# A layer's first panels: the third low part ahead of the folding of the squares, the ones-matmul and the turn of the roots one panel later

## What is computed

```python
def rms_norm_2(x, gain, eps=NORM_EPS):
    xf = x.astype(jnp.float32)
    y = xf * lax.rsqrt(jnp.mean(xf * xf, axis=-1, keepdims=True) + eps)
    return (y * gain.astype(jnp.float32)).astype(x.dtype)
...
    h = x
    for l in range(DEPTH_2):
        u = rms_norm_2(h, attn_norm[l])
        proj = jnp.einsum('bsd,dc->bsc', u, w_in[l])
        (dq, dk, dv, rq, rk, rv, rg, gq, gk, gv, gate_logits) = split_cols(proj, IN_SPLITS)
...
        h = h + jnp.einsum('bsd,de->bse', merged, w_out[l])
        m = jnp.einsum('bsd,df->bsf', rms_norm_2(h, mlp_norm[l]), w_mlp_in[l])
        m = jnp.square(jax.nn.relu(m))
        h = h + jnp.einsum('bsf,fd->bsd', m, w_mlp_out[l])
```

## Time and profile before

| | |
|---|---|
| time, median of 3 runs | 2093.12 us (2092.78 to 2095.03) |
| time of the profiled execution | 2092.37 us |
| its span | 2090.3 us |
| TensorE busy | 1963.7 us, 94% of the span |
| VectorE, GpSimd, ScalarE busy | 54%, 29%, 19% |
| mean granted clock of TensorE | 0.982 |

### The profile page before, as it was taken

One profiled execution on the slowest core, in us unless ns is written; L12 is line 12 of the kernel. 1 busy time (PEld: TensorE's weight loads), 2 busy tenths in 40 slices (PEclk: granted clock), 3 DMA queues, 4 the chain that ended last, 5 costly groups with the idle time before them and its releaser, 6 DMA issues.

```text
span 2090.3 us, 33307 instructions
## 1 busy us (share of the span) xinstructions
PE 1963.7 (94%) x13854; PEld 1776.9 (85%) x13854; DVE 1133.7 (54%) x1205; ACT 392.1 (19%) x724; POOL 601.3 (29%) x505
## 2 busy tenths in 40 slices
PE   6989999999998878899999999889999999889999
PEld 3548888788998867899998998689999999689999
DVE  1342222333447987654466776675546677576554
ACT  1320100011222231111122112511112112432110
POOL 0011222122134721333333332123333332124332
PEclk9999999999999989999999999999999999999999
DMA  9694222222233221445444343145554434234552
GB/s 356 222 351 183 89 92 100 101 96 86 81 112 141 82 100 62 145 155 185 182 163 161 142 141 142 61 145 181 183 185 173 161 137 147 81 124 171 184 184 104
DMA packets 43515, 307.84 MB, mean 147 GB/s; under 512 B 5072, under 2 KB 5456, under 8 KB 6608
## 3 DMA queue, kind: packets, MB, share of 16 engines
q1 hardware_dynamic: 40752, 292.66, 38.8%
q10 hardware_dynamic: 2656, 13.58, 1.7%
HBM read 303.08 MB, written 3.15 MB: 146 GB/s over the span
## 4 chain that ended last, share of the span: by engine, by line
PE 79%; DVE 11%; issue 4%; POOL 2%; ACT 2%; DMA 2%; SPq 0%; DVEq 0%; POOLq 0%; ACTq 0%
PE ps L1704 23%; PE ps L1706 22%; PE ps L1705 22%; DVE wlo L604 2%; POOL whi L531 2%; PE ps L1878 2%; DMA landing<-in_stream 2%; PE ps L1866 1%; PE ps L2101 1%; PE ps L2008 1%; PE ps L1829 1%; PE ps L2125 1%; DVE xlo L664 1%; PE ps L1794 1%; PE ps L1968 1%
## 5 line engine op out<-in xcount | busy, mean ns | idle before, releaser
L1704 PE MATMUL ps<-xhi,whi 128*128 128x256 f32 (+1 forms) x3680 | 1115.7, 303 | 35.1 <-DVE xlo L612 21.4
L1705 PE MATMUL ps<-xlo,whi 128*128 128x256 f32 (+1 forms) x3680 | 1103.0, 300 | 0.0
L1706 PE MATMUL ps<-xhi,wlo 128*128 128x256 f32 (+1 forms) x3680 | 1102.8, 300 | 0.0
L604 DVE TENSOR_TENSOR wlo<-landing,whi 128x2048 fp32r<-128x2048 f32 x242 | 562.2, 2323 | 456.8 <-POOL whi L531 456.4
L1704 PEld LDWEIGHTS ps<-xhi,whi 128*128 128x128 f32 x3680 | 709.7, 193 | 69.0 <-issue 30.6
L1705 PEld LDWEIGHTS ps<-xlo,whi 128*128 128x128 f32 x3680 | 709.8, 193 | 22.4 <-issue 1.0
L1706 PEld LDWEIGHTS ps<-xhi,wlo 128*128 128x128 f32 x3680 | 709.2, 193 | 20.7
L530 POOL TENSOR_TENSOR whi<-landing,ones 128x128 fp32r<-128x128 f32 x242 | 125.1, 517 | 1465.4 <-PE ps L1706 1316.1
L531 POOL TENSOR_SCALAR whi<-landing 128x1920 fp32r<-128x1920 f32 x242 | 442.3, 1828 | 0.0
L792 DVE TENSOR_TENSOR big<-big,ps 128x512 f32 (+3 forms) x44 | 24.4, 555 | 200.1 <-ACT big L1355 200.1
L1367 ACT ACTIVATE xhi<-big 128x512 fp32r (+3 forms) x66 | 45.8, 696 | 386.0 <-PE ps L1706 332.8
(11 more groups left out here) (252 smaller groups left out, 1414.1 us busy)
## 6 DMA issues: line engine op xcount, KB each, us to landing
landing<-in_stream SPq DMA_DIRECT2D x278, 1024.0 KB, 4.8
spectra<-big ACTq DMA_DIRECT2D x2, 1024.0 KB, 10.1
ws<-spectra ACTq DMA_DIRECT2D x2, 1024.0 KB, 4.7
ws<-in_tabs ACTq DMA_DIRECT2D x1, 1280.0 KB, 5.7
ws<-in_hyc ACTq DMA_DIRECT2D x1, 1024.0 KB, 19.4
h<-in_xT ACTq DMA_DIRECT2D x1, 1024.0 KB, 23.8
ws<-in_ctxT ACTq DMA_DIRECT2D x1, 1024.0 KB, 31.4
ws<-in_lbrow ACTq DMA_DIRECT2D x1, 1024.0 KB, 14.7
```

Source lines behind the costliest of these rows:

```text
L604: v.tensor_tensor(wlo[:, s % 2], landing[:, s], whi[:, s % 2].bitcast(F32), ALU.subtract).then_inc(lo_done, 1)
L1704: mm(out, w_hi, x_hi, start=first, stop=False, skip_group_check=True)
L1705: mm(out, w_hi, x_lo, start=False, stop=False, skip_group_check=True)
L1706: return mm(out, w_lo, x_hi, start=False, stop=last, skip_group_check=True)
```

## The change

On VectorE the fold moves behind one more low part, and for layer 0 the first scales move with it. On TensorE the ones-matmul comes after p2 instead of after p1, and the turn of the roots after p3 instead of after p2, where it now stands directly ahead of `lam_sums` and p4. No instruction is added or taken away.

```diff
@@ -1073,9 +1073,9 @@
                             dve.wait_ge(inv_done, 2 * l + 1)
                         evict(i - 1)
                     low_next(i)
-                    if i == 0:
+                    if i == 1:
                         fold(2 * l, 2 if l == 0 else 1)
-                    if i == 1 and l == 0:
+                    if i == 2 and l == 0:
                         first_scales()
                     if i == 2:
                         lam_parts()
@@ -2080,9 +2080,9 @@
 
                 for i in range(N_HEADS):
                     proj(i)
-                    if i == 1:
+                    if i == 2:
                         boundary_sums(2 * l)
-                    if i == 2:
+                    if i == 3:
                         turn_rstd()
                     if i == 3:
                         lam_sums()
```

## The result

| | before | changed |
|---|---|---|
| median of 11 runs each | 2093.61 us (2092.70 to 2098.41) | 2097.60 us (2096.15 to 2101.98) |
| ratio | | 1.002, 95% interval 1.0011 to 1.003 |
| span of the profiled execution | 2090.3 us | 2095.4 us |
| mean granted clock of TensorE | 0.982 | 0.969 |

The changed kernel is slower by 4 us, where 2.7 us of gain were forecast. That is just the 0.2% named at the start, but the interval lies wholly above 1. The time is above the range, which ended at 2092.9.

What follows compares the result with a forecast made beforehand. TensorE, busy 94% of 2090.3 us, bounds the kernel, so only its idle and half-clock time at the doors could go. Layer 0 gives 3.74 us, layer 1 loses 1.07: 2.7 less, forecast 2090.4 us, range 2088.6 to 2092.9.

Steps and rivals of the forecast that it cites:

- what happens in layer 0: At layer 0's door, gaps ahead of p2 go, smaller waits come ahead of p3 and p4; gain 3.74 us.
- The wait ahead of p4: In each layer, p4 directly behind the turn and `lam_sums` must wait; a new cost of 1.08 us.
- GpSimd gets ahead of p3's low part: Layer 0: GpSimd's two instructions come first, making p3's gap 3.6 us; 2092.7, or 2094.2 with half clock; chance 0.15.
- I take no loss: TensorE's clock behind the new gaps ahead of p3 and p4: nothing lost, at most 1.35 to 1.7 us each.
- The prediction's own sign of being wrong: In the profile after, a stretch at 0.50 of the clock inside p3 or p4 would be wrong.
- slower: half clock behind the new waits: Waits ahead of p4 in both layers and p3 in one each bring a 1.6 us stretch: 2095.2; chance 0.07.
- from two such stretches on: Two half-clock stretches behind the new waits give 2093.6, above the median of 2093.12, so the change loses.
- one stretch lost: At a later door, one more stretch of half clock: 2092.0; chance 0.1.

Runs made afterwards that it cites:

- e4: The kernel before with only the turn of the roots moved from behind p2 to behind p3, in both layers; 2107.13 us, ratio 1.0069.
- e2: The changed kernel with p4's sums in PSUM bank 7, so p4 need not wait for the values of p0; 2096.66 us, ratio 1.0012.
- e1: The changed kernel with p4 multiplied over all 256 columns of its panel instead of 128; 2094.23 us, ratio 1.0.
- g2: The kernel before with the turn moved behind p3 and p4 multiplied over all 256 columns; 2097.49 us, ratio 1.0012.
- f4: The new order in layer 1 alone, layer 0 as in the kernel before; 2101.12 us, ratio 1.0039.
- e3: The new order in layer 0 alone, layer 1 as in the kernel before; 2090.85 us, ratio 0.9986.
- f1: The changed kernel with the turn of the roots between the two halves of p3, in both layers; 2090.55 us, ratio 0.9989.
- f2: The changed kernel with p4's sums in PSUM bank 7 and p4 multiplied over all 256 columns; 2091.66 us, ratio 0.9987.
- f3: The new order in layer 0 alone, with the turn between the halves of p3 there; layer 1 as before; 2091.36 us, ratio 0.999.

## Why the prediction was wrong

**Right, nearly to the tenth: what happens in layer 0.** Less the 1.25 us of later start, the ones-matmul began at 1103.58 (forecast 1103.59), p3's low part was issued at 1103.31 (1103.28), p3 began at 1105.65 (1105.62), the turn at 1111.60 (1111.56) and p4 at 1113.42 (1113.31). The gain was 3.63 us where 3.74 was forecast. The wait ahead of p4 lengthened the way by 1.02 us in layer 1, where 1.08 was forecast.

**Right: the rival "GpSimd gets ahead of p3's low part" did not come.** The low part was issued 0.52 us before GpSimd's turn; 0.6 was forecast. The Trainium skill ("SBUF — State Buffer", Who interferes with whom) says that for the shared port the order of issue decides which of the two engines has to wait. The trace agrees: the later one, GpSimd's L530, took 2.09 us instead of 0.46.

**Wrong: "I take no loss; the other end is one stretch, 1.35 us (p2's lengthening) to 1.7 (half of 3.40) for each gap."** This term of the sum, the clock behind the new waits, was set to nothing, and it measured 4.8 us in layer 1 of the changed kernel and in each layer of e4. The prediction's own sign of being wrong, a stretch at 0.50 inside p4, is what came. Two things were wrong in it. I compared only idle times, and put p4's wait beside others that kept the full clock. But those stood between matmuls of 256 and 512 columns; here the turn, `lam_sums` and the wait stand directly ahead of the one narrow panel, and e2 shows that there the clock can fall with no idle time at all. And the bound of one stretch was taken from places where wide matmuls follow. Behind p4's wait narrow ones follow: at half clock they start 0.21 us apart instead of 0.11, and the clock came back only in p5. e1 and g2, which differ from the changed kernel and from e4 in the width alone, had 3.4 us and none at all.

**The rival "slower: half clock behind the new waits" was the one that happened**, with a chance of 0.07 and the price of a stretch, 1.6 us, too low by a factor of three. It put the loss at "from two such stretches on"; one was enough, since one was worth 4.8 us. The range left this rival out, even at its own price of 2095.2. Its upper end, 2092.9, took in no more than GpSimd ahead (2092.7) or one stretch lost (2092.0).

**Left out: that p4 differs from the panels ahead of it.** The `128x128` in the row of its first matmul and the `n = COLS if i < 4 else P` of the code both say so. Moving the turn took away p3, 5.8 us of wide matmuls, from between two thin pieces of work.

**Open.** In which layer the clock falls is not settled. With the new wait and the narrow p4, layer 1's fell in all four profiles that had them (changed, e4, f4, and e2 without the idle time), layer 0's in e4 alone and not in the changed kernel, e2 or e3. The moment differs too: layer 0's p4 starts 23.2 to 24.2 us behind the clock's last return to 1.00 in the changed kernel, e2 and e3, and 11.8 us behind it in e4, whose gaps ahead of p2 brought a stretch of half clock of their own. Whether it is that moment or those gaps that let layer 0 fall in e4, no run separates. Neither explains away what the experiments showed of the width and the thin work. In layer 1 the moments of e4, f4 and e1 are alike (210.5, 210.5 and 210.7 us, with 10.2, 10.2 and 3.4 us of half clock), and so are those of e2, f1 and f2 (209.2, 209.4 and 209.5 us, with 10.2, none and none). g2's, at 236.1 us, has no like among them, so what g2 shows is shown by layer 0. Of the wait and the small matmuls as causes, e2 shows the latter to be enough in layer 1; a wait alone was not tried. The gain of f1 and f3 stayed about 1 us below the 4.6 us of the removed gaps, of which 0.8 us was traced in f1.

The new order itself is good, if by little: with the turn inside p3 (f1) the kernel takes 0.9989 (0.998 to 0.9998) of before's time, and less than the changed kernel. The profile's rest shows 3.5 us.

## What to carry to other kernels

Before a small matmul or a wait is moved on TensorE, look at what stands on both sides of its new place. Here 0.8 us of thin work directly ahead of a panel with half the columns cost up to 5.8 us, 4.8 of them because the granted clock fell and did not come back within that panel. With wide matmuls behind it, as in f2, the same work cost nothing of the kind. A price for half clock has to be taken from a place where the same kind of matmul follows, not only the same length of idle time. And split a change that moves several things: one line of this one cost 12 us by itself in the kernel before, and the others gained about 3.

## What the runs showed of the hardware

- The granted clock fell from 1.00 to 0.50 behind a stretch of 3.30 us in which TensorE was busy all the time (e2), with matmuls of 2 and of 128 columns in it.
- In all five falls at a narrow p4 (changed, e2 and f4 in layer 1, e4 in both) the clock stayed at 0.50 for 10.2 us with TensorE busy throughout. In none of the five did it come back while matmuls of 128 columns ran; it came back 2.0 to 4.6 us after those of 256 columns had begun.
- A narrow p4 alone is not enough: in the kernel before, in f1 and in f3 both p4 ran at 1.00 throughout, with the turn of the roots elsewhere.
- Matmuls of 128 columns start 0.11 us apart at full clock and those of 256 columns 0.12. At half clock both start 0.21 us apart. So a narrow matmul saves nothing worth having here, and it nearly doubles in price when the clock falls.
